# Two small tiles to the front, a filling and a shorter constants tile: new byte positions for the SBUF buffers of a two-layer hybrid decoder

## What is computed

```
h = rms_norm(x, norm1_g);  proj = h @ w_in            # 1024 x 2560
retention (4 heads), block-sparse attention (4 heads), attention into rms_norm(mem) @ w_mem_kv (4 heads)
x = x + concat(y_ret, y_moba, y_mem) @ w_out           # 1024 x 1024
t = rms_norm(x, norm2_g)
# top-1 group of 4, then top-2 of its 4 experts: 2 of 16 experts per token
for e in 16 experts: out += combine[:, e] * ((silu(t @ w_gate[e]) * (t @ w_up[e])) @ w_down[e])   # 1024 x 512, 512 x 1024
x = x + out
```

## Time and profile before

| what | value |
|---|---|
| median of 3 runs | 1177.26 us (1176.79 to 1181.42) |
| the profiled execution's own time | 1175.16 us |
| its span, first to last instruction | 1173.2 us |
| mean granted TensorE clock | 0.977 |
| busy share of the span: PE, DVE, ACT, POOL | 94%, 76%, 62%, 14% |
| moved by DMA | 275.18 MB, mean 235 GB/s |
| instructions | 18117 |

### The profile page before, as it was taken

One profiled execution on the slowest core, in us unless ns is written; L12 is line 12 of the kernel. 1 busy time (PEld: TensorE's weight loads), 2 busy tenths in 40 slices (PEclk: granted clock), 3 DMA queues, 4 the chain that ended last, 5 costly groups with the idle time before them and its releaser, 6 DMA issues.

```text
span 1173.2 us, 18117 instructions
## 1 busy us (share of the span) xinstructions
PE 1099.4 (94%) x5563; PEld 909.2 (77%) x5563; DVE 895.3 (76%) x1339; ACT 729.7 (62%) x1039; POOL 161.3 (14%) x234
## 2 busy tenths in 40 slices
PE   5999999999999999999689999999999999999990
PEld 4887888788788888888568878878878888888870
DVE  4469777557998989989574777683699899898973
ACT  4735533325888888888454454441388888888860
POOL 2000402001011110110310005200011101111011
PEclk9999999998999999999799999999899999999995
DMA  9422111219999879999673121121599996999965
GB/s 338 160 90 72 55 54 64 90 49 335 373 367 386 327 278 384 374 381 356 249 243 105 57 91 54 64 74 53 193 342 367 382 367 236 376 371 379 381 240 225
DMA packets 121361, 275.18 MB, mean 235 GB/s; under 512 B 13233, under 2 KB 13473, under 8 KB 121168
## 3 DMA queue, kind: packets, MB, share of 16 engines
q1 hardware_dynamic: 106976, 240.32, 56.4%
q0 software_dynamic: 14320, 34.09, 7.9%
HBM read 267.48 MB, written 23.07 MB: 248 GB/s over the span
## 4 chain that ended last, share of the span: by engine, by line
PE 79%; DVE 13%; DMA 4%; issue 2%; ACT 2%; POOL 0%; SPq 0%; POOLq 0%; DVEq 0%; ACTq 0%
PE bank L1478 22%; PE bank L1480 21%; PE bank L1479 21%; DVE w_lo L428 2%; PE bank L1839 2%; PE bank L1510 2%; PE bank L1696 1%; PE bank L1858 1%; PE bank L1742 1%; PE bank L1637 1%; PE bank L1631 1%; DMA hd<-pair_rows 1%; DMA act<-pair_rows 1%; DVE proj L1058 1%; PE bank L1789 1%
## 5 line engine op out<-in xcount | busy, mean ns | idle before, releaser
L422 DVE TENSOR_TENSOR w_lo<-stage,w_hi 128x1024 fp32r<-128x1024 f32 x244 | 294.2, 1222 | 15.9 <-ACT w_hi L417 14.4
L417 ACT ACTIVATE w_hi<-stage 128x1024 fp32r<-128x1024 f32 x236 | 246.5, 1059 | 48.0 <-PE bank L1480 48.0
L1478 PE MATMUL bank<-w_hi,hT_hi 128*128 128x512 f32 x384 | 156.5, 408 | 5.3 <-DVE hT_lo L1015 4.0
L1480 PE MATMUL bank<-w_hi,hT_lo 128*128 128x512 f32 x384 | 150.3, 391 | 0.0
L1479 PE MATMUL bank<-w_lo,hT_hi 128*128 128x512 f32 x384 | 149.9, 390 | 0.0
L422 DVE TENSOR_TENSOR more_lo<-stage,more_hi 128x1024 fp32r<-128x1024 f32 x124 | 146.2, 1220 | 2.4 <-ACT more_hi L417 1.4
L417 ACT ACTIVATE more_hi<-stage 128x1024 fp32r<-128x1024 f32 x124 | 128.0, 1061 | 15.2 <-PE bank L1480 14.6
L428 DVE SCALAR_TENSOR_TENSOR w_lo<-stage,g_cols,w_hi 128x512 fp32r<-128x512 f32 x96 | 68.6, 765 | 51.4 <-ACT w_hi L382 49.8
L1478 PE MATMUL bank<-w_hi,xgT_hi 128*128 128x512 f32 x264 | 104.8, 397 | 1.1 <-DVE xgT_lo L1376 1.1
L1480 PE MATMUL bank<-w_hi,xgT_lo 128*128 128x512 f32 x264 | 104.3, 395 | 0.0
L1479 PE MATMUL bank<-w_lo,xgT_hi 128*128 128x512 f32 x264 | 104.2, 395 | 0.0
(11 more groups left out here) (265 smaller groups left out, 2027.5 us busy)
## 6 DMA issues: line engine op xcount, KB each, us to landing
stage<-in_w_exp_up SPq DMA_DIRECT2D x124, 512.0 KB, 6.3
stage<-in_w_exp_gate SPq DMA_DIRECT2D x122, 512.0 KB, 6.4
stage<-in_w_exp_down SPq DMA_DIRECT2D x122, 512.0 KB, 6.3
stage<-in_w_in SPq DMA_DIRECT2D x40, 512.0 KB, 5.1
stage<-in_w_out SPq DMA_DIRECT2D x16, 512.0 KB, 3.9
stage<-in_w_mem_kv SPq DMA_DIRECT2D x8, 512.0 KB, 6.8
h_scratch<-act POOLq DMA_DIRECT2D x8, 512.0 KB, 3.2
act<-pair_rows POOLq DMA_DIRECT2D x8, 512.0 KB, 6.4
```

The source lines that it names most:

```text
L417: eng.activation(x_hi[n % NX], src, ACT.Copy).then_inc(s_hi, 1)
L422: eng.tensor_tensor(x_lo[n % NX], src, x_hi[n % NX].bitcast(f32), ALU.subtract).then_inc(s_lo, 1)
L1478: pe.matmul(dst, l_hi, r_hi, start=start, stop=False)
L1480: return pe.matmul(dst, l_lo, r_hi, start=False, stop=stop)
```

## The change

The tiles `rstd` (64 bytes in a partition) and `lg` (320 bytes) move ahead of `x`. The parts of `con` are put in another order, so that the two unread ones come last, and the tile and its load end before them (2204 columns in place of 2340). A filling of 96 bytes, which nothing reads or writes, stands behind the last small tile. No instruction of an engine is added, removed or moved; one load is shorter.

```diff
-             iota=16, pairid=8, empty=128, limits=3)
+             iota=16, limits=3, pairid=8, empty=128)
...
+N_LIVE = OFF["pairid"]
...
+        rstd = sb("rstd", [128, 16])
+        lg = sb("lg", [128, NT, 20])
         x = sb("x", [128, NT, D])
         stage = sb("stage", [128, NS, D])
...
-        con = sb("con", [128, N_CONST])
+        con = sb("con", [128, N_LIVE])
...
-        rstd = sb("rstd", [128, 16])
...
-        lg = sb("lg", [128, NT, 20])
...
         pair_now = sb("pair_now", [128, 2, 1], i32)
+        sb("to_512", [128, 24])
...
-                    sp.dma_start(con[:, N_FIRST:], a["const_pack"][:, N_FIRST:]).then_inc(s_const, 16)
+                    sp.dma_start(con[:, N_FIRST:], a["const_pack"][:, N_FIRST:N_LIVE]).then_inc(s_const, 16)
```

## The result

The changed kernel took 1169.57 us (median of 4 runs, 1165.12 to 1170.14), the kernel before 1178.62 us beside it (median of 4, 1176.79 to 1181.42): ratio 0.9904, 95% interval 0.988 to 0.9929, so 8.4 to 14.1 us less. The forecast was 1164.0 with a range of 1158 to 1178. The profiled execution took 1170.14 us, its span 1168.2 us; that of the kernel before 1175.16 and 1173.2.

The account below looks back on a forecast made before the run. PE bounds the kernel, busy 94% of the span. Gains and losses, 15.2 - 2.4 + 0.4 + 0.2 - 0.3 = 13.1 us, off 1175.2 gave 1162.1; with 2.1 for the median, 1164 us, range 1158 to 1178.

Parts of the forecast that it names:

- The theory of the place: 512-column matmuls: pace depends on the two operands' relative place by 512 bytes; equal remainders give 226.7 ns, unequal up to 233.3.
- slower: Rival: the stationary buffer's own place sets the pace and 0 is bad; hT's matmuls fall to 233.3 ns; 1185 us, chance 0.07.
- no change: Rival: pace depends on which part of memory a buffer stands in, so small shifts do nothing; 1177 us, chance 0.17.
- better than equal: Rival: at remainder 0 both streams start on a boundary and pace falls to 220 ns; 1156 us, chance 0.07.
- (a): Expert matmuls: 2304 of them go from 233.3 to 226.7 ns, 15.2 us gained on PE's path.
- (b): Expert steps: after transposes interrupt, the fast pace isn't there at once; 2.4 us of the expert gain not reached.
- (c): Output projection from wx: 192 matmuls go from 228.9 to 226.7 ns, 0.4 us gained.
- (e): Constants' load at the start: 70 KB shorter, so the w_in loads queued behind it come sooner; 0.2 us gained.
- (f): Late expert weight loads: DMA has no rate left, only slack, so a faster PE loses 0.3 us, between 0 and 2.2.
- one sign that I had named for "right": End of an expert pass: weight loads land later than 7.7 us with PE still busy without a gap.
- Rule against the change: All matmuls: independent SBUF read ports mean places could not matter; the whole gain would be 0.2 us.

Follow-up runs that it names:

- both groups at 448: Against the kernel before: x through the projection's buffers, and wx, mk, xgT, hidT and those among them, at remainder 448 by 512 bytes; 1171.88 us, ratio 0.9922.

## Why the prediction was right, and where it was off

- **The theory of the place was right.** Pace goes with the relative place, equal remainders give 226.7 ns. The kernel with both groups at 448 rules out "slower" (own place of the stationary buffer) and "no change" (region of the memory); "better than equal" did not come at 0, 128 or 448. What was wrong is the period: 256 bytes, not 512. The cause that the prediction gave below it, a weight load and a stream that read the same memory in turns, was not tested.
- **(a) and (b), 15.2 less 2.4.** The step was forecast at 17.72 us and is 17.70. The kernel with Silu's table ahead of the loop gained 270.1 + 270.0 - 263.6 - 263.4 = 13.1 us between the first and the 16th group of the two passes. Of this 0.8 us is what the loads had cost before (0.27 + 2 x 0.07 in each pass), which leaves 12.3 us in 30 of the 32 steps, beside 12.8 forecast for all.
- **Missing term: the table loads.** The changed kernel itself gained only 11.2 us there. The prediction doesn't name the six loads, so they stood in it at nothing. The slower matmuls had covered most of them, and a quicker PE lays them bare: 1.9 us in place of 0.8, so 1.1 us. The row I read, had ACT busy for 15.32 of 18.10 us, but that was a step without a load; a load adds 1.28.
- **(c), 0.4.** 2.5 ns each by the table above (229.2 less 226.7), 0.3 to 0.4 us in the traces. Right.
- **(e), 0.2.** Not to be told from 0.
- **(f), 0.3 lost.** In the changed kernel nothing was lost to late loads. I took the DMA's rate as used up and its slack as the cover, but the rate rose by 9 GB/s. So one sign that I had named for "right" did not come: loads landing later than 7.7 us at the end of a pass (6.5 us from 500 to 550 us in the changed kernel run again). Nothing was lost because the change moved `stage` too, which the forecast had not priced: that the small figure came out nearly right is luck. With `stage` at 128 or 448 the shortage is real and costs 3.7 to 4.1 us by the medians (2.7 us at 128 and 3.8 at 448 in the two expert passes together), more than my upper bound of 2.2; at 0 or 256 it is none. The rule of the Trainium skill that I had set beside the rivals ("DMA: Bandwidth & Descriptors", section "How a descriptor splits into AXI transactions") has the first transaction of a descriptor that doesn't start at a multiple of 256 bytes begin at the boundary below and fetch bytes that are not used. The traces agree in this: places 0 and 256 land in time, 128 and 448 don't. It should have been a term of (f). But the page tells it of what a transaction reads, and the runs moved only the target of these transfers: that the rule is the cause of what they show for writes into SBUF is argued, not shown.
- **Missing term: VectorE and GpSimd.** A meeting of the two that fell well for DVE before and badly after: 1.5 us in two layers. This was bad luck: no row of before could foretell a lead of 0.01 us in place of 0.06; what could be seen is that they met.
- **Rule against the change.** The Trainium skill, "TensorE: Matmul & The Clock Gate", section "Step-by-step: what each phase is for", has loads of weights on a read port of their own. The measurements decide: 226.7 to 233.3 ns for the same instruction with nothing but the distance changed.
- **Sum.** 13.1 - 1.1 - 1.5 = 10.5, plus 0.3 for (f), is 10.8 us; measured 9.1 and 12.2 at the medians, 11.7 between two profiles at one clock. Of the 5.6 us between 1164.0 and 1169.57 that explains 2.3; 1.4 more is the base, 1178.62 beside the changed kernel where the forecast stood on 1177.26 (1178.3 to 1181.8 in the later sets); the remaining 1.9 lies within the interval of the ratio and has no term.

Left open: what makes the pace depend on the distance; why at distance 0 the matmuls behind an interruption reach the pace only at the eleventh start (227 to 233 ns in the mean before it, in the changed kernel's expert runs), while at distance 64 they go at 233 to 234 from the second on; and why a lead of 0.05 us is enough for VectorE and one of 0.03 is not.

## What to carry to other kernels

Give the moving and the stationary buffer of long fp32r matmul chains the same remainder by 256 bytes, and place the buffers that a full DMA queue writes at a multiple of 256; a filling or a small tile put elsewhere is all it takes, and here it was worth 1%. Read the pace as the distance of starts over some twenty matmuls: a few ns from one line's run to another's is a cause to look for. When PE gets quicker, go through what it used to cover, table loads in loops first, and compare two profiles only at equal granted clock.

## What was not expected of the hardware

- The pace has a period of 256 bytes in the operands' distance and depends on its sign: 226.7, 233.3, 232.9, 229.2 ns at 0, 64, 128, 192.
- Transfers of 4 KB a partition into a buffer at 0 or 256 landed after 6.4 to 8.0 us (medians of `gate` units, 500 to 550 us) in steps of 17.7 us, at 387 to 389 GB/s (450 to 540 us); at 128 or 448 after 8.7 and 8.9, at 383 and 380.
- A DVE instruction of 0.74 us took 1.67 us when a GpSimd instruction started with it or at most 0.03 us behind it; when DVE was 0.05 us or more ahead, it kept its 0.74 and the GpSimd one took 1.66 in place of 1.1.
